# Seven block products in the MLP's first product for the second pair of tiles, with the weight sums kept in DRAM

## The reference

```
h = rmsnorm(x, norm_mix[i]);  x = x + mixer(h)        # A, B, C, A for i = 0..3
x = x + channel_mlp(rmsnorm(x, norm_mlp[i]), m_w1[i], m_w2[i])
def channel_mlp(h, w1, w2):
    return jnp.square(jax.nn.relu(h @ w1)) @ w2       # (2048,1024) @ (1024,4096), (2048,4096) @ (4096,1024)
```

## Time and profile before

| | |
|---|---|
| runs (3) | median 3122.33, lowest 3119.52 us |
| profiled execution | 3120.32 us, its span 3118.8 us |
| cores' spans | 3109.1 to 3118.8 us, granted TensorE clock 0.993 to 0.996 |
| TensorE / VectorE / ScalarE / GpSimd busy | 98% / 68% / 38% / 20% |
| DMA | 331.60 MB, of them 298.61 MB on GpSimd's queue |

### The profile page before, as it was taken

The page is one execution under the profiler, slowest core; times in us unless marked ns, Lnnn a source line. Parts: engine busy times, 40 slices in busy tenths (PEclk is TensorE's granted clock), DMA queues, the critical chain, the costliest instruction groups (busy, mean ns, idle before and its releaser), DMA issues.

```text
span 3118.8 us, 46054 instructions; the slowest of 8 cores (3109.1 to 3118.8 us)
## 1 busy us (share of the span) xinstructions
PE 3049.2 (98%) x15253; PEld 1473.4 (47%) x15546; DVE 2130.7 (68%) x3804; ACT 1184.3 (38%) x2013; POOL 616.0 (20%) x683
## 2 busy tenths in 40 slices
PE   8999999999999999999998999999999999999998
PEld 4444444444444444444576444444444444444444
DVE  7945756566778966666658797757755757466765
ACT  4312433444434343443534512342322333434434
POOL 1111233001102410100551500101212141200300
PEclk9999999999999999999999999999999999999999
DMA  9599897444447424454422444447897987644553
GB/s 169 103 156 167 160 167 128 85 80 83 74 72 130 73 49 82 82 116 77 106 47 82 70 87 81 80 76 127 137 166 132 159 141 134 110 82 82 104 110 85
DMA packets 100841, 331.60 MB, mean 106 GB/s; under 512 B 7040, under 2 KB 10240, under 8 KB 100608
## 3 DMA queue, kind: packets, MB, share of 16 engines
q0 software_dynamic: 83424, 298.61, 56.4%
q1 hardware_dynamic: 17184, 30.02, 3.2%
HBM read 613.56 MB, written 13.63 MB: 201 GB/s over the span
## 4 chain that ended last, share of the span: by engine, by line
PE 93%; DMA 2%; DVE 2%; issue 2%; ACT 1%; another core or an unknown queue 0%; POOL 0%; SPq 0%; DVEq 0%; ACTq 0%; POOLq 0%
PE bank L164 93%; DMA ring<-m_w 1%; DMA xT<-x 1%; DVE xT L164 0%; DMA ring<-b_w_in 0%; DVE m_tv L164 0%; DMA ring<-a_w_in 0%; ACT ring L164 0%; DVE ring L164 0%; DVE b_pl L164 0%; ACT sq L164 0%; ACT m_tv L164 0%; DVE hall L164 0%; ACT rs L164 0%
## 5 line engine op out<-in xcount | busy, mean ns | idle before, releaser
L164 DVE TENSOR_TENSOR xT<-bank,xT 128x512 f32<-128x512 f32 (+2 forms) x1120 | 735.7, 680 | 325.7 <-PE bank L164 291.6
L164 PE MATMUL bank<-m_tv,ring 128*128 128x512 bf16 (+2 forms) x3653 | 792.8, 373 | 12.3 <-DVE xT L164 8.2
L164 PEld LDWEIGHTS bank<-m_tv,ring 128*128 128x128 bf16 x3724 | 359.3, 98 | 430.9 <-issue 19.6
L164 ACT ACTIVATE bank<-bank 128x512 f32<-128x512 f32 x448 | 260.8, 582 | 658.2 <-PE bank L164 640.3
L164 DVE TENSOR_TENSOR m_tv<-m_tv,m_tv 128x512 bf16<-128x512 bf16 x494 | 211.3, 448 | 339.6 <-ACT m_tv L164 338.3
L164 POOL DMA_DIRECT2D ring<-m_w x192 | 115.8, 603 | 1344.3 <-PE bank L164 1329.3
L164 ACT ACTIVATE m_tv<-bank 128x512 bf16<-128x512 f32 x511 | 304.5, 597 | 163.7 <-DVE bank L164 122.8
L164 POOL TENSOR_TENSOR sacc<-sacc,sq 128x512 f32<-128x512 f32 (+1 forms) x180 | 232.2, 1290 | 164.4 <-ACT sq L164 100.8
L164 DVE TENSOR_TENSOR ring<-ring 128x512 bf16<-128x512 bf16 x496 | 211.0, 444 | 47.9 <-DMA ring<-m_w 37.5
L164 ACT ACTIVATE sq<-xT 128x512 f32<-128x512 f32 (+1 forms) x252 | 153.8, 619 | 219.2 <-DVE xT L164 105.9
L164 PE MATMUL bank<-hall,ring 128*128 128x512 bf16 x1003 | 223.7, 379 | 1.1
(11 more groups left out here) (211 smaller groups left out, 3747.1 us busy)
## 6 DMA issues: line engine op xcount, KB each, us to landing
ring<-a_w_in POOLq DMA_DIRECT2D x88, 1024.0 KB, 13.6
ring<-m_w POOLq DMA_DIRECT2D x64, 1024.0 KB, 8.5
ring<-m_w POOLq DMA_DIRECT2D x128, 512.0 KB, 5.1
ring<-a_w_out POOLq DMA_DIRECT2D x64, 768.0 KB, 7.6
xT<-x SPq DMA_DIRECT2D x16, 512.0 KB, 11.5
ring<-b_w_in POOLq DMA_DIRECT2D x8, 1024.0 KB, 15.4
out<-xT SPq DMA_DIRECT2D x12, 512.0 KB, 8.5
x_spill<-xT SPq DMA_DIRECT2D x4, 1280.0 KB, 15.1
```

The lines of the kernel that those rows point to most:

```text
L164: return lambda e: getattr(e, _method)(*[_r(a) for a in args], **{k: _r(v) for k, v in kwargs.items()})
```

## The change

In the second pair of tiles the MLP's first product is also made with seven block products (`G1s`): 28 matmuls for a unit in place of 32. The combinations of h for it are made once for each layer (`hsums`, four sums of 128x2048 on VectorE). After three of the products ScalarE copies the bank to SBUF (`copy`), and VectorE adds this copy into other banks (`out`).

`m_w1` is laid out in 16 units of 2048 elements like `m_w2`, each in a slot of its own. In the first pair VectorE makes the weight sums in the slot for both products (`wsums`: 512, 1024 and 512 elements), and SP's queue stores 3584 elements of each partition to `m_pre` in DRAM (`keep`). In the second pair SP's queue reads them back (`load_pre`): there are no f32 loads and no weight sums there.

Around it: the two adds to x behind `G2`'s last product become one of 128x1024 (`add_both`); in block (1, 3) the adds of two products go by a copy on ScalarE and an add on GpSimd (`RELIEF`, `add_pool`); `G1` of the first block of the second pair is moved behind `G2` of block (0, 3), and that of (0, 3) ahead of it; the next mixer's squares begin at (1, 0) (`pre_steps`) and its h at (1, 3); after mixer C, only the first block uses the unscaled h with the scale in the ReLU; at the end of mixer B tile 1's squares wait for the last pooled value (`hold`), and the last two pooled values get their own buffers; the cost of a bf16 sum in the scheduler goes from 0.09 to 0.18 us plus its length.

```diff
-        din("m_w1", (4, 8, 128, 4096))
+        din("m_w1", (4, 16, 128, 2048))
...
+        m_pre = nc.dram_tensor("m_pre", [2, 16, 128, 3584], BF16, kind="Internal").ap()
+        pre_r = [[Res() for _ in range(16)] for _ in range(2)]
...
+    def add_both(dc, tt, bk):
+        out = xT[:, dc, tt * 512:(tt + 2) * 512].rearrange("p (a c) -> p a c", a=2)
+        sc.op("dve", I("tensor_tensor", out=out, in0=bk.v(lambda t: t[:].unsqueeze(1).broadcast_to([128, 2, 512])), in1=out, op=ALU.add),
+              rd=[bk], wr=[xr(dc, tt), xr(dc, tt + 1)], cost=c_dve(1024), tag="xadd")
+    def add_pool(dc, tt, bk, tmp):
+        t, r = tmp
+        sc.op("act", I("activation", out=t, in_=bk.v(), func=AF.Copy), rd=[bk], wr=[r], cost=c_act(), tag="xcopy")
+        sc.op("pool", I("tensor_tensor", out=xs(dc, tt), in0=xs(dc, tt), in1=t, op=ALU.add), rd=[r], wr=[xr(dc, tt)], cost=c_pool(),
+              port=True, tag="xaddp")
...
+    RELIEF = ("A11", "A12")
...
-        return 0.09 + n / 1900.0
+        return 0.18 + n / 1900.0
...
+                hn[tt] = mix_h4(tt + 2)
...
-                rs = rms(tt, (rsx_[0][0][:], rsx_[0][1][0]) if tt >= 2 else None, mode)
+                rs = rms(tt, (rsx_[0][0][:], rsx_[0][1][0]) if tt >= 2 else None, mode, after=hold if tt == 1 else ())
...
+        def load_raw(name, idx):
+            t, r, key = take_slot()
+            last_load[0] = sc.op("pool", I("dma_start", out=t[:, 0:2048], in_=dram[name][l, idx], max_dma_last_dim=8192), wr=[r],
+                                 cost=0.95, dma=key, nbytes=512 * 2048, tag="load")
+            w_ops.append(last_load[0])
+            return (t,) + views(t, r)
+
+        def load_pre(kind, idx):
+            t, r, _ = take_slot()
+            sc.op("sp", I("dma_start", out=t[:, 512:4096], in_=m_pre[kind, idx]), rd=[pre_r[kind][idx]], wr=[r],
+                  cost=0.06, dma=pre_key[slot_of(t)], nbytes=256 * 3584, tag="pre")
+            v, vr = views(t, r)
+            return four(v), vr
+
+        def wsums(t, v, vr):
+            comb(v["T1"], [vr["T1"]], v["W12"], [vr["W12"]], v["W11"], [vr["W11"]], ALU.subtract)
+            comb(t[:, 2560:3584].rearrange("p (a c) -> p a c", a=2), [vr["n3"], vr["n2"]],
+                 v["W22"].unsqueeze(1).broadcast_to([128, 2, 512]), [vr["W22"]],
+                 t[:].rearrange("p (a b c) -> p a b c", a=2, b=4)[:, :, 0, :], [vr["W12"], vr["T1"]], ALU.add, 1024)
+            comb(v["T4"], [vr["T4"]], v["W21"], [vr["W21"]], v["n2"], [vr["n2"]], ALU.subtract)
+
+        def keep(kind, idx, t, vr):
+            if not (last and kind and idx >= 12):
+                sc.op("sp", I("dma_start", out=m_pre[kind, idx], in_=t[:, 512:4096]), rd=[vr[k] for k in QUADS[1:]],
+                      wr=[pre_r[kind][idx]], cost=0.06, dma=st_key[slot_of(t)], nbytes=256 * 3584, tag="keep")
+
...
         def G1(p, b, i):
-            if i % 2 == 0:
-                w1[(p, b, i // 2)] = load_w("m_w1", l, b * 2 + i // 2, (32, 128))
-            w, wr_ = w1[(p, b, i // 2)]
+            if p:
+                G1s(p, b, i)
+                return
+            t_, v, vr = load_raw("m_w1", b * 4 + i)
+            if b:
+                h.update(hn)
+                hn.clear()
+                rst.clear()
...
+            wsums(t_, v, vr)
+            keep(0, b * 4 + i, t_, vr)
...
+        def hsums():
+            (h0, r0), (h1, r1) = h[3], h[2]
+            H["A11"], H["A12"] = (h0[:, 0:4, :], r0[0:4]), (h0[:, 4:8, :], r0[4:8])
+            H["A21"], H["A22"] = (h1[:, 0:4, :], r1[0:4]), (h1[:, 4:8, :], r1[4:8])
+            for j, k in enumerate(("S1", "m2", "n4")):
+                t, r = zone("m_h", (128, 4, 512), BF16, h_off + 4 * KB * j)
+                H[k] = (t[:], r)
+            H["m3"] = H["A21"]
+            for o, x, y in (("S1", "A21", "A22"), ("m2", "A11", "S1"), ("m3", "A21", "A11"), ("n4", "A12", "m2")):
+                comb(H[o][0], H[o][1], H[x][0], H[x][1], H[y][0], H[y][1], ALU.subtract, 2048)
+            H["temps"] = [zone("m_s", (128, 512), F32, h_off + (12 + 2 * j) * KB) for j in range(2)]
+            H["temps"] = [(t[:], r) for t, (r,) in H["temps"]] + [(b[0][:], b[2]) for b in sqb]
+        def temp():
+            sn[0] += 1
+            return H["temps"][sn[0] % len(H["temps"])]
+        def G1s(p, b, i):
+            w, wr_ = load_pre(0, b * 4 + i)
+            a, f, e, g = Bank(), Bank(), Bank(), Bank()
+
+            def prod(bk, hk, wk, start):
+                mm = MM if start else MORE
+                sc.op("pe", [mm(bk.v(), w[wk][:, k, :], H[hk][0][:, k, :], start and k == 0, k == 3) for k in range(4)],
+                      rd=[wr_[wk]] + H[hk][1], wr=[bk], cost=c_pe(4), tag="W1")
+
+            def copy():
+                t, r = temp()
+                sc.op("act", I("activation", out=t, in_=a.v(), func=AF.Copy), rd=[a], wr=[r], cost=c_act(), tag="part")
+                return t, r
+
+            def out(bk, src, s, k):
+                sc.op("dve", I("tensor_tensor", out=bk.v(), in0=src.v(), in1=s[0], op=ALU.add), rd=[s[1]] + ([] if bk is src else [src]),
+                      wr=[bk], cost=c_dve(), tag="cadd")
+                relu(bk)
+                square(bk, p, b, i, k)
+
+            prod(a, "A11", "W11", True)
+            s1 = copy()
+            prod(f, "A12", "W21", True)
+            out(f, f, s1, "A21")
+            prod(a, "m2", "n2", False)
+            s2 = copy()
+            prod(e, "m3", "n3", True)
+            prod(a, "S1", "T1", False)
+            s4 = copy()
+            out(a, e, s4, "A12")
+            prod(g, "n4", "W22", True)
+            out(g, g, s4, "A22")
+            prod(e, "A22", "T4", False)
+            out(e, e, s2, "A11")
 
...
-            w, wr_ = load2(b, d)
+            if p:
+                w, wr_ = load_pre(1, b * 4 + d)
+            else:
+                t_, v, wr_ = load_raw("m_w2", b * 4 + d)
+                wsums(t_, v, wr_)
+                keep(1, b * 4 + d, t_, wr_)
+                w = four(v)
...
-                for dc, tt in outs:
-                    add_to_x(dc, tt, bk)
+                if len(outs) == 2:
+                    add_both(*x12, bk)
+                elif relief and ak in relief:
+                    xn[0] += 1
+                    add_pool(*outs[0], bk, xtemp[xn[0] % len(xtemp)])
+                else:
+                    add_to_x(*outs[0], bk)
...
-        early = [prep(tt, "pool") for tt in range(2)]
-        yield early
+        hold = []
+        early = [prep(tt, "dve" if raw_first else "pool") for tt in range(2)]
+        yield early, hold
         for e in early:
             run_all(e)
         pipe = [(p, b) for p in range(2) for b in range(4)]
         for i in range(H_BLK):
             G1(0, 0, i)
             sums(0, 0, i)
+        for tt in hn:
+            rmsnorm(tt, gcol, *hn[tt], rs=rst[tt])
         for j, (p, b) in enumerate(pipe):
             more = j + 1 < len(pipe)
+            plain = last and not more
+            turn = b == 2
             if (p, b) == (0, 0):
                 work.extend(prep(tt, "pool") for tt in (2, 3))
             if (p, b) == (1, 0):
-                work.extend(gen_store(tt) if last else nxt.after_steps(tt) for tt in (0, 1))
+                work.extend(gen_store(tt) if last else nxt.pre_steps(tt) for tt in (0, 1))
             if (p, b) == (1, 3) and not last:
-                work.extend(iter(nxt.late_steps(tt)) for tt in (0, 1))
-            while (p, b) == (0, 3) and work:
+                work.extend(iter(f(tt)) for f in (nxt.after_steps, nxt.late_steps) for tt in (0, 1))
+            while (p, b) == (0, 2) and work:
                 step()
             for i in range(H_BLK):
-                plain = last and not more
-                if more and i < H_BLK - 1:
+                ahead = more and (i < H_BLK - 1 or turn)
+                if (p, b) == (1, 3):
+                    step(4)
+                if ahead and (p, b) != (0, 3):
                     G1(*pipe[j + 1], i)
+                    if (p, b) == (0, 2) and i == H_BLK - 1:
+                        hsums()
                 if not plain:
                     G2(p, b, i)
                 elif i == 0:
...
                         step()
                     plain_block(p, b)
                 if more:
-                    if i == H_BLK - 1:
+                    if not ahead or (p, b) == (0, 3):
                         G1(*pipe[j + 1], i)
                     if not (last and j + 2 == len(pipe)):
                         sums(*pipe[j + 1], i)
...
+                    if tt == NT - 1 and g >= 2:
+                        po, po_r = zone(f"b_pe{g}", (128, 2, 512), BF16, 16 * KB + 2 * W * 4 * ((tt * 4 + g + 2) % NP), 2)
...
+                    if tt == NT - 1 and g == 3:
+                        hold.append(o)
...
+        def pre_steps(self, tt):
+
+            run, (run_r,) = rsb[tt]
+            self.pre[tt] = (run, run_r)
+            for k, kc in enumerate(KORDER[:-1]):
```

(40 more changed lines are left out.)

105 lines of the change are left out of this document (58 added, 47 removed).

## The result

The changed kernel took **3143.23 us** (median; 3141.8 to 3151.8 undisturbed) against 3119.52 for the kernel before in the same job: ratio **1.0082 [1.0065, 1.0099]**. It is slower by 0.8%, which lies within the 2% that count as the same, and 78 us above the forecast. In the profiled execution the cores' spans are 3123.6 to 3141.4 us. In some executions of every kernel here the cores of one die run at a lower granted clock and take some per cent longer; the ratios and the runs called undisturbed leave these out.

The account below looks back on a forecast made before the run. TensorE was taken as the bound: matmuls times 0.2155 us plus border losses. 3120.3 - 55.2 (matmuls removed) + 6.2 (copies' links) - 6 (mixer B's end) gave 3065 us, with an 8-in-10 range of 3046 to 3090.

Parts of the forecast that it names:

- Cost: 0 while this cover stands: DMA in first pairs: share rises from 0.45 to 0.87 with two loads and two stores a unit, costing nothing.
- Cost: 0: VectorE's added work: net +138 us, about 74% busy, costing TensorE nothing; bounds -5 to +12 us.
- late sums of weights on VectorE: Sign of being wrong: first pairs lose their pace through DMA or through these late sums; no size given.
- The copies' links: G1s in second pairs: 52 links with just 4 matmuls cost 0.12 us each, +6.2 us; bounds 0 and 12.
- Matmuls removed: First product of the second pair: 256 fewer matmuls at 0.2155 us each on TensorE, -55.2 us.
- Mixer B's end: Late last pooled values there no longer idle TensorE: -6 us; bounds -7.7 (all) and +2 (moved norm becomes a wait).
- Other borders: Remaining moves at borders between stages, such as norm work, G1 order, ReLU scheme and relief adds: 0, with -8 to +8 us.
- More borders heal: Rival, chance 0.28: most of the 12.8 us lost at three borders outside mixer B's end goes, giving 3049 us.
- Waits of accumulation in the second pair: Rival, chance 0.14: late ScalarE or VectorE queues delay reused G1s banks, +32 us, 3097, with many short TensorE waits.
- First pair bound by DMA: Rival, chance 0.04: two stores beside two loads make a first-pair unit 17.0 us, +262 us, giving 3327.

Follow-up runs that it names:

- u2_borders: Changed kernel with the second pair's first product plain, weights summed again there and nothing stored, so only the border moves stay; ratio 1.0086 to the kernel before.
- e2_late: Changed kernel with the scheduler's plan landing each load of m_w1 and m_w2 5 us later, nothing else; ratio 0.9975 to the kernel before.
- e5_late_link: Changed kernel with weight loads planned 5 us later and G1s copies costed 0.2 us higher; 3077.72 us, ratio 0.9887 to the kernel before.
- e1_sliver: Changed kernel with stores to m_pre writing 256 of 3584 elements per partition (second-pair weights wrong); ratio 0.9929 to the kernel before.

## Why the prediction was wrong

**The step that failed** is the DMA's "Cost: 0 while this cover stands", with VectorE's "Cost: 0" beside it. The load itself was about right: where first pairs keep their pace the DMA share is 0.84 to 0.90 (0.75 to 0.78 in the last layer) for 0.87 worked out, and VectorE has 132 us more for 138. Both conclusions came from plain averages: a share of 1.02 and one of 93% had cost TensorE nothing. But in the first of these stretches VectorE has no sums of fresh weights in its order, and in the second the DMA share was 0.48 and none of the 18 sums waited for its load. In first pairs VectorE's order has such sums between adds to x, now of both products' weights, and stores beside the loads moved the landing from 5.1 to 8.4 us. That the order stands on landings could be seen in the trace of before, where VectorE waited 54 times, 37.5 us in all, for `m_w`. Such waits do not measure the cost: in u2_borders they are 69.4 us in 50, and TensorE's for adds to x stay at 6.7. With the later landings they grew to 160.9 us, and TensorE's for adds to x from 8.2 to 48.4. I named "late sums of weights on VectorE" as what would make me wrong, and gave it no price.

Its size: in the four first-pair stretches of 180, 200, 200 and 205 us core 0 issued 750 + 867 + 807 + 872 = 3296 loads where before it issued 834 + 927 + 913 + 949 = 3623. 327 x 0.2155 = 70 us; on core 3, 244 loads, 53 us. The 55.2 us saved were given back there. Of the 70 us, 55.5 are idle time of TensorE; for the rest it was busy at a mean granted clock of 0.96 to 0.99 in these stretches, where it had 1.00. And in the stretch from 1750 some 7 us are due to a border move (the 34 loads of u2_borders), not to the stores. That e2_late and e5_late_link have the loads back with the same bytes shows the cause; that e1_sliver has most of them back without any edit to the planner shows the trigger.

**The copies' links** (+6.2, upper bound 12) were mis-sized. A link was sized about right (0.12, 0.14 measured); there are more of them than 52. 546 loads instead of 556 in 120 us is 1.8% of some 760 us of second pairs: 14 us at most, 10 on core 0 by its three such windows (546, 548, 548 against 556, 556, 552). That is 70 to 100 links of 0.14 us; the late starts of e2_late, core 4, in its three windows are 34 in 360 us, 72 in 760. With longer links 2 to 4 loads are missing, 3 to 5 us.

**Matmuls removed**, -55.2: right. e5_late_link shows it: 3120.3 - 55.2 + 3 (554 of 556) + 5 (its waits at borders, 21.9 against 16.9) = 3073, and it ran at 3077.7, its spans 3068 to 3077.

**Mixer B's end**, -6: the place healed, with 47 records in 1070 to 1080. But in the changed kernel the norm moved behind became a wait, as the bound of +2 had it, and took most of the gain:

```profile
1107.76 8.82 DVE L164 SCALAR_TENSOR_TENSOR mh1v<-xT,pv,rs 128x512 bf16<-128x512 f32 x8 [2.62 <-ACT rs L164]
...
1116.73 5.46 PE L164 MATMUL bank<-mh1v,ring 128*128 128x512 bf16 x17 [4.19 <-DVE mh1v L164]
```

From 1040 to 1140 the kernel before issued 428 loads (core 4), the changed one 436 and 431 (cores 0 and 3): a gain of 8 and 3 loads, 0.6 to 1.7 us. In u2_borders and e5_late_link, core 4 and core 0, no wait over 0.8 us stands there and the loads are 464 and 461, 7 to 8 us more than before. So this wait hangs on the order that the planner gave, not on the edit. The eight products took 1.10 us each, those for tile 0 at 1082 even 1.62 (11.33 us for 7), with GpSimd adding squares most of the while; in e5_late_link at 1740, with GpSimd idle beside them, eight took 0.67 each. The Trainium skill's exclusive port pair (SBUF — State Buffer, SBUF: two separate sides) would have it so; these rows agree in kind, without showing the single locks. By it the term was to be the whole -7.7, since squares no longer run beside the pooled values; that came true, and the squares, which still have to be made, now slow the norm products.

**Other borders**, 0: right in sum by the waits (1 us in u2_borders) and wrong in kind, since old waits went and new ones came, one of them with 28 us of lower clock behind it on some cores of that kernel. The edit that most needed a price of its own is the one behind mixer C: with the factor kept behind the product for one block only, 16 products of 0.67 us fall on VectorE between two blocks, and TensorE waits for them, 3.4 us in the changed kernel, 4.4 in e5_late_link, 5.5 in u2_borders.

**The rivals.** More borders heal: no. Waits of accumulation in the second pair: not as named. The many short waits behind VectorE's adds did not come; the 10 to 14 us that second pairs lost are the copies' links of the sum, with no wait listed. First pair bound by DMA: no. It ran whole in e2_late and e5_late_link with the same transfers. The loss in first pairs that I gave to this rival alone, at 262 us, came by another way at 53 to 70.

## What to carry to other kernels

Where each engine runs a fixed order, ask of every added transfer not only whether the DMA engines have room, but how much later the loads beside it will land, and which instruction in an order stands on that landing; a listed wait of an engine that is not the bound shows which instruction that is, though not what it costs. Before a structural saving is judged, set the planner's landing times and link costs to what the changed traffic makes them: here two numbers were worth 65 us, more than the 55 that the change was to save. And count what a step moves as a wait to look for elsewhere.
